# Expert stage: gathers and mixing tiles of the pair ahead in one stretch between up and down products

## The reference

```python
expert = (g_idx[:, None] * EXPERTS_PER_GROUP + top_i).reshape(-1)   # 2 of 32 experts a token
order = jnp.argsort(expert); tok = order // TOP_K
xs = xf[tok]
h = silu(ragged_dot(xs, w_gate, sizes)) * ragged_dot(xs, w_up, sizes)
y = ragged_dot(h, w_down, sizes) * weights.reshape(-1)[order][:, None]
out = segment_sum(y, tok, num_segments=T)
```

## Time and profile before

| | |
|---|---|
| median of 3 runs | 1879.24 us (1878.63 to 1880.14) |
| the profiled execution's own time | 1881.57 us |
| its span, first to last instruction | 1879.8 us |
| TensorE busy | 1845.2 us, 98% |
| VectorE busy | 857.5 us, 46% |
| ScalarE busy | 558.5 us, 30% |
| GpSimd busy | 101.2 us, 5% |
| HBM read | 483.31 MB |
| gate and up products, L1185, share of the chain that ended last | 23% |
| down products, L1209 | 11% |
| gathers, L1150 | 6% |
| mixing, L1171 | 6% |

### The profile page before, as it was taken

The page is one execution under the profiler, slowest core; times in us unless marked ns, Lnnn a source line. Parts: engine busy times, 40 slices in busy tenths (PEclk is TensorE's granted clock), DMA queues, the critical chain, the costliest instruction groups (busy, mean ns, idle before and its releaser), DMA issues.

```text
span 1879.8 us, 22187 instructions
## 1 busy us (share of the span) xinstructions
PE 1845.2 (98%) x9046; PEld 1166.4 (62%) x9046; DVE 857.5 (46%) x1382; ACT 558.5 (30%) x1015; POOL 101.2 (5%) x144
## 2 busy tenths in 40 slices
PE   8999999999999999999899999999999999999997
PEld 7875778686444444544588888787684444544543
DVE  4566564536333433433433455465363433433433
ACT  4436353634111111111344442445351111111110
POOL 2200010001000000000000022001010000000000
PEclk9999999999999999999999999999999999999999
DMA  6210243137999999999633322342159999999997
GB/s 238 90 68 23 90 135 110 47 118 302 401 420 420 420 421 419 420 420 420 239 124 109 116 76 82 112 135 90 48 224 368 420 420 420 419 420 420 420 420 296
DMA packets 99672, 486.92 MB, mean 259 GB/s; under 512 B 8224, under 2 KB 8336, under 8 KB 53872
## 3 DMA queue, kind: packets, MB, share of 16 engines
q1 hardware_dynamic: 97440, 479.23, 64.2%
q0 software_dynamic: 1456, 5.14, 0.9%
q10 hardware_dynamic: 672, 1.07, 0.2%
HBM read 483.31 MB, written 2.10 MB: 258 GB/s over the span
## 4 chain that ended last, share of the span: by engine, by line
PE 92%; DVE 3%; DMA 2%; ACT 2%; issue 0%; POOL 0%; DVEq 0%; POOLq 0%; ACTq 0%
PE ps L741 28%; PE ps L1185 23%; PE ps L1209 11%; PE ps L738 7%; PE ps L1150 6%; PE ps L1171 6%; PE ps L1101 1%; DMA slot<-in_moe_w_down 1%; PE ps L969 1%; DMA ring<-in_c_w_in 1%; PE ps L1082 1%; PE ps L791 1%; PE ps L1245 1%; PE ps L1030 1%; DVE wl L605 1%; PE ps L1192 1%
## 5 line engine op out<-in xcount | busy, mean ns | idle before, releaser
L1185 PE MATMUL ps<-ring,xg 128*64 128x512 f32 x1040 | 261.4, 594 | 3.3 <-DMA ring<-in_moe_w_up 3.3
L605 DVE SCALAR_TENSOR_TENSOR wl<-ring,gcols,wh 128x512 fp32r<-128x512 f32 x200 | 148.9, 750 | 204.3 <-ACT wh L591 202.9
L741 PE MATMUL ps<-wh,ah 128*128 128x512 f32 x544 | 216.2, 397 | 5.5 <-DVE wl L605 3.1
L1185 PE MATMUL ps<-slot,xg 128*64 128x512 f32 x848 | 219.0, 594 | 0.0
L741 PE MATMUL ps<-wh,al 128*128 128x512 f32 x544 | 212.2, 390 | 0.0
L741 PE MATMUL ps<-wl,ah 128*128 128x512 f32 x544 | 212.0, 390 | 0.0
L2437 DVE SCALAR_TENSOR_TENSOR hh<-ps,columns_of,sg 128x512 f32<-128x512 f32 x32 | 36.2, 1131 | 367.0 <-PE ps L1185 367.0
L591 ACT ACTIVATE wh<-ring,gcols 128x512 fp32r<-128x512 f32 x200 | 142.2, 719 | 205.8 <-PE ps L741 161.1
L2458 DVE TENSOR_TENSOR x<-ps,x 128x1024 f32<-128x1024 f32 x120 | 144.1, 1222 | 83.5 <-PE ps L1171 79.7
L1185 PEld LDWEIGHTS ps<-ring,xg 128*64 128x64 f32 x1040 | 82.7, 137 | 145.5 <-issue 145.2
L1185 PEld LDWEIGHTS ps<-slot,xg 128*64 128x64 f32 x848 | 68.9, 137 | 120.4 <-issue 120.4
(11 more groups left out here) (344 smaller groups left out, 2888.5 us busy)
## 6 DMA issues: line engine op xcount, KB each, us to landing
ring<-in_moe_w_up SPq DMA_DIRECT2D x68, 1024.0 KB, 13.5
slot<-in_moe_w_down SPq DMA_DIRECT2D x68, 1024.0 KB, 18.9
ring<-in_moe_w_gate SPq DMA_DIRECT2D x62, 1024.0 KB, 16.1
slot<-in_moe_w_gate SPq DMA_DIRECT2D x54, 1024.0 KB, 11.3
slot<-in_moe_w_up SPq DMA_DIRECT2D x52, 1024.0 KB, 17.0
ring<-in_moe_w_down SPq DMA_DIRECT2D x50, 1024.0 KB, 13.9
ring<-in_x_wkv SPq DMA_DIRECT2D x16, 1024.0 KB, 5.1
ring<-in_c_w_in SPq DMA_DIRECT2D x16, 1024.0 KB, 5.2
```

The lines of the kernel that those rows point to most:

```text
L605: dve.scalar_tensor_tensor(out=wl[:, t % STAGE, :], in0=ring[:, SLOT[unit], 512 * s:512 * (s + 1)], scalar=g, in1=wh[:, t % STAGE, :].bitc ...
L741: mm = pe.matmul(ps[:, b + m, :], a[:, (k + k0) % steps, m * P:(m + 1) * P], w[:, (t0 + k) % STAGE, :], **flags)
L1185: mm = pe.matmul(ps[p * SLOTS:(p + 1) * SLOTS, bank, :], xg[:, b % 2, k, r * P + p * SLOTS:r * P + (p + 1) * SLOTS], w(p)(k % 4), start=(k ...
```

## The change

- TensorE: behind the up product now stand the first gather, mixing tiles 0 and 1 of the pair ahead, the transposes, tiles 2 and 3 of the pair ahead, and the second gather; then the two parts of the down product, and at once the next pair's gate product. Tile 0 uses `MIX`, 1 `Y`, 2 `MIX`, 3 `Y`, so that tile 2 waits for tile 0's addition and tile 3 for tile 1's, and the down product waits for all four.
- ScalarE copies the second gather ahead of the down product's results. VectorE does all four additions of the pair ahead in a row.
- Last pair: `split_next` behind the results (ScalarE) and behind the last additions (VectorE).
- Routing: two idle products ahead of the four small products.

```diff
                 b = begin(("logits", l, 0))
+                idle_products(2, 2)
...
-                        if m >= 2 and bank != GATE:
-                            pe.wait_ge(S["y_added"], 4 * (q0 + q) + 4 - m)
+                        if m >= 2:
+                            pe.wait_ge(S["y_added"], 4 * (q0 + q) + m - 1)
...
                     if part == 0:
                         pe.wait_ge(S["hT_ready"], q0 + q + 1)
-                        after(pe, S["y_added"], 4 * (q0 + q) - 1)
+                        after(pe, S["y_added"], 4 * (q0 + q))
...
-                    if more or q == 2 * b:
-                        do_hidden(q, GATE, 0)
+                    do_hidden(q, GATE, 0)
...
                     if more:
                         do_gather(b + 1, 2 * (q % 2), GATHER)
                     if q:
-                        do_mix(q - 1, 2, Y)
+                        do_mix(q - 1, 0, MIX)
+                        do_mix(q - 1, 1, Y)
                     pe.wait_ge(S["h_ready"], q0 + q + 1)
                     after(pe, S["hT_ready"], q0 + q)
                     hidden_T().then_inc(S["hT_done"], 1)
                     if q:
-                        do_mix(q - 1, 3, MIX)
+                        do_mix(q - 1, 2, MIX)
+                        do_mix(q - 1, 3, Y)
+                    if more:
+                        do_gather(b + 1, 2 * (q % 2) + 1, GATHER)
                     if q + 1 == PAIRS:
                         last_down(q)
                         last_mix(q)
                         return
                     do_down(q, 0)
                     do_down(q, 1)
-                    if more:
-                        do_gather(b + 1, 2 * (q % 2) + 1, GATHER)
-                    else:
-                        do_hidden(q + 1, GATE, 0)
-                    do_mix(q, 0, MIX)
-                    do_mix(q, 1, Y)
...
                     hidden_copy().then_inc(S["hT_ready"], 1)
+                    if more:
+                        gathered(b + 1, 2 * (q % 2) + 1, GATHER)
                     after(act, S["mixed"], 4 * (q0 + q))
                     if q + 1 == PAIRS:
-                        if l + 1 < LAYERS:
-                            act.wait_ge(stage_used, STAGES * (q0 + q) + 4)
-                            split_next()
                         act.wait_ge(S["half_down"], l + 1)
                         result_hi(0).then_inc(S["yh_ready"], 1)
                         act.wait_ge(stage_used, STAGES * (q0 + q + 1))
                         result_hi(1).then_inc(S["yh_ready"], 1)
+                        if l + 1 < LAYERS:
+                            split_next()
...
                     if q:
-                        do_add(q - 1, 2, Y)
-                        do_add(q - 1, 3, MIX)
+                        do_add(q - 1, 0, MIX)
+                        do_add(q - 1, 1, Y)
+                        do_add(q - 1, 2, MIX)
+                        do_add(q - 1, 3, Y)
                     if q + 1 < PAIRS:
                         slot_rows(q + 1)
-                    if q + 1 == PAIRS and l + 1 < LAYERS:
-                        dve.wait_ge(stage_used, STAGES * (q0 + q) + 4)
-                        split_next()
                     for half in range(2):
                         dve.wait_ge(S["yh_ready"], 2 * (q0 + q) + half + 1)
                         result_lo(half).then_inc(S["y_split"], 1)
                     if q + 1 == PAIRS:
                         last_adds(q)
+                        if l + 1 < LAYERS:
+                            split_next()
                         return
-                    do_add(q, 0, MIX)
-                    do_add(q, 1, Y)
```

More of the change, by code:

```diff
@@ L1820, in pair @@
                             result_hi(half).then_inc(S["yh_ready"], 1)
-                    if more:
-                        gathered(b + 1, 2 * (q % 2) + 1, GATHER)
                 for block in range(4):
```

## The result

| | median (lowest to highest), us | ratio to before, same chip | profiled span |
|---|---|---|---|
| before | 1879.32 (1878.24 to 1880.14) | 1 | 1879.8 |
| after | 1884.32 (1882.98 to 1885.25) | 1.0025 [1.0017, 1.0032] | 1882.6 |

Both medians are of 12 runs. The change makes the kernel 5.0 us slower; I had forecast 1.6 us. The profiled spans lie only 2.8 us apart: the profiled execution of before (1881.57 us) was slower than all of its 12 runs, and carried a fall of the clock that a second profile doesn't have (experiment 1).

What follows compares the result with a forecast made beforehand. Expert stage: TensorE and weight transfers are limits 3% apart, the weights' last landing setting its end. Terms +2.1 + 0.4 - 0.2 + 0 - 0.8 + 0.1 = +1.6 us on the median 1879.24 give 1880.8 us; range 1875.5 to 1886 us.

Steps and rivals of the forecast that it cites:

- the second hole: Weight transfers near 502 us: a late release opens a gap of 1.5 to 2 us in the loads.
- the fourth rival: Last pairs: the clock falls after TensorE idles before the down product, up to 1.7 us, twice; 1884 us, chance 0.10.
- TensorE's +0.4: Expert stage: TensorE reaches the last up product 0.4 us later per layer; +0.4 us taken in the sum.
- the landings' -0.2: Expert weights' transfers: the last landing comes 0.1 us sooner a layer, bounds -2 to +1.5; -0.2 us in the sum.
- The clock's -0.8: Layer 0's routing: two more idle products keep the full clock, worth 1.6 us, of which half was taken.
- Switches and waits in the stretch: Ordinary pairs: one excursion fewer saves 0.3 us, waits for additions cost 0.42 us; 29.2 us a pair.
- the rival of arriving gains: Whole kernel: the additions' waits and second transfer gap don't exist, so the savings show; 1871 us, chance 0.12.
- TensorE never became the bound: Rival, expert stage: TensorE bounds, the last up product is reached 4 to 5 us later; 1887 us, chance 0.15.
- Pairs 14 and 15: Pairs without gathers: the down product starts 6.3 us after the first mixing product, 1.6 us of it waiting.
- The first hole: Weight transfers at 480 us: a gap of 2.3 us that closes but for little, its release coming 2.6 us sooner.
- The end of layer 1: Pair 15 of layer 1: the last down product and everything behind it come 2.1 us later; +2.1 us.
- The end of layer 0: Last down product 3.5 us later, but splits fill VectorE's idle time before the next layer's low halves; sum 0 (-1 to +1).

Runs made afterwards that it cites:

- experiment 1: The kernel before, unchanged, profiled once more (also called before again or before repeated); 1879.91 us, ratio 1.0001.
- Experiment 5: The changed kernel with the order of before in pairs 14 and 15, the rest of the change kept; 1877.08 us, ratio 0.9983.
- experiments 2: The kernel before with only the two idle products ahead of the small routing products added; 1879.74 us, ratio 1.0000.
- experiment 4: The kernel before with only the last pair's results put ahead of the weight splits; 1878.93 us, ratio 0.9997.
- Experiment 8: The changed kernel without TensorE's branch over the overflow passes, the other engines keeping theirs; 1881.97 us, ratio 1.0010.
- experiments 6 and 7: The kernel before (6) and the changed kernel (7), loading half of each unit of the down weights' second part from pair 2 on; 1869.73 and 1875.39 us.
- kernels 9 and 11: The kernels of experiment 5 (9) and experiment 4 (11) with layer 0's TensorE branch ahead of the last pair's up products; 1879.53 and 1876.80 us.

## Why the prediction was off

The time, 1884.3, lies in the range, 3.5 us above the forecast. Two terms of the sum failed, both to the same side, and it is luck that the range, drawn wide for other reasons (the second hole, a later last up product), still took them in. That the fourth rival's time was 1884 us is chance as well. By the traces, experiment 1 against the changed kernel (us, start of each event in both):

| event | before again | after | step | predicted |
|---|---|---|---|---|
| last up product, layer 0 | 893.53 | 893.83 | +0.3 | +0.1 |
| last mixing, layer 0 | 909.87 | 910.64 | +0.5 | +0.8 |
| first turn behind it | 916.79 | 918.51 | +0.9 | |
| first dense product | 920.50 | 923.09 | +0.9 | -0.8 with the line above |
| first gate product, layer 1 | 1406.46 | 1408.71 | -0.3 | 0 |
| last up product, layer 1 | 1851.71 | 1854.12 | +0.2 | +0.1 |
| end | 1877.71 | 1882.62 | +2.5 | +2.1 |

(Steps are the growth of the difference since the line above; TensorE's +0.4 and the landings' -0.2 are shared out over the layers. The clock's -0.8 and the idle products' +0.1 are in no line; neither trace has the fall in the routing. By the prediction's own argument that the landings decide, TensorE's +0.4 should have counted for nothing.)

**Switches and waits in the stretch: right as a sum.** 29.08 us a pair for 29.2, tile 2 at 4.30 (4.4), tile 3 at 5.43 (5.5), the second gather at 6.47 (6.55), the down product at 8.33 (8.45). The saving and the waits cancel, so the rival of arriving gains falls. The 64 gate and up products take 13.73 us for 13.88, so a part of the saving shows by itself; the rest was seen only together with the waits. TensorE never became the bound either: it waits 5.4 us for up weights, more than before.

**Pairs 14 and 15: right.** A down product 6.23 us behind the first mixing product for 6.3, 1.36 us idle for 1.6. The clock didn't fall there: the fourth rival named the wrong place.

**The transfers: right.** The first hole closed, a second opened at 500 us, and the last up weights of layer 0 landed within 0.3 us of before. The release came at 500.62, where I had put 502.0.

**The end of layer 1: right in kind,** 2.5 us for 2.1. Experiment 5 shows that it is the order of the last two pairs: there the last down product follows the last up product of layer 1 by 1860.90 - 1851.06 = 9.84 us, in the changed kernel by 13.28.

**The clock in layer 0's routing: failed, 0.8 us.** I took half of a fall that only one execution had; the base of the runs had none. The idle products had nothing to give back.

**The end of layer 0: failed, some 2 us.** I had put its sum at 0: the last mixing 0.8 us later, and then "the splits fill VectorE's idle time". The last mixing came as forecast, and so did the additions (they end 6.3 us behind its start, for 6.2). But the chain behind it is not VectorE's. The turns wait for TensorE's own branch, which I had left out. It starts with the end of the second low half and takes 6.2 us; from that end to the turns are 6.4 to 6.5 us in the first trace, in before repeated, in experiments 2, 4 and 5 and in the changed kernel. The sign was in the first trace (the turns start 0.46 us behind the additions, "issue"), and I read it as a latency.

The path I had in mind gave back the 2.73 us wait and the low clock of the last mixing. Neither was there to be had. In experiments 1 and 2 the first ten mixing products take 2.57 us (granted clock 1.00) and 4.13 us (0.58 from 910 to 914 us), and the turns start at 916.79 and 916.75 us all the same. And the second low half follows the late last down product: it ends at 912.07 us for 910.32, 1.75 later, and the turns start 1.72 later. TensorE idles 3.9 us for 3.0, the clock falls, and the turns take 3.57 us for 1.94. Experiment 8 shows the branch, experiment 4 what moving the splits does by itself.

Without the clock's -0.8 and with the measured 2.0 us of layer 0's end (0.5 + 1.8 - 0.3) the forecast would have been 1.6 + 0.8 + 2.0 = +4.4 us, against 5.0.

## What to carry to other kernels

Tie two producers into one stretch where enough other work stands in it to hide their consumer, and keep the old order in the last rounds, where it doesn't: here the ordinary pairs cost nothing (29.08 us a pair for 29.09), and the last ones made the whole loss. Before a wait is removed, look for what else the next step waits for, jumps among it: "issue" with nothing else to wait for is a cost with an owner. And take a second profile of the old kernel before a fall of the clock in one execution is put into the sum.

## What the hardware showed

A taken branch over a long body on TensorE took 6.1 to 6.3 us while weights streamed in, 3.9 and 3.4 us at the same place with lighter transfers (experiments 6 and 7), and 3.3 to 4.0 us behind layer 1. A packet of 16 KB on an instruction queue ran within it, 3.6 to 3.7 us after its start beside the weights and 1.0 us in the light kernels. TensorE stood still when its queue had run dry within it, 2.8 us in kernels 9 and 11.

After 3.9 to 4.0 us of idleness ahead of the turns the clock fell in each trace that has them, and the turns took 2.5 to 3.7 us for 1.94. The stretch of the changed kernel in which they run:

```profile
918.50:921.50 3.00, 2.99 (x14) 3.00 (x15) 0.44 (x1) 1.01 (x1) 0.00 (x0) 0.50 0.05 14
```

The granted clock is 0.50, its lower level of 1.2 GHz. After 2.8 us idle (kernels 9 and 11) it fell in one kernel and not in the other; after the 3.00 us of before repeated it didn't fall, and after 2.24 us in the light changed kernel it did (0.56 from 916.6 to 920.5 us). The Trainium skill ("TensorE: Matmul & The Clock Gate", Part 1) has the lower clock as the default that activity lifts; the falls behind idle stretches agree, and these four cases show that the length of the last idle stretch alone doesn't settle it.
